# Moving a sample's and a recurrence's start to slots without weight splitting, transposing all first token pairs on TensorE, and starting the cache copies later

## The reference

```python
xn = _rmsnorm(x, g_pre)
u = xn @ w_in
gq, gk, gv, gg, glr, dq, dk, dv, dg, ga, gb = jnp.split(u, cuts, axis=-1)
# branch A: gated linear attention, in chunks of 64 tokens
b = jnp.cumsum(a_, axis=1)
q_in = q_ * jnp.exp(b)
att = jnp.where(causal, jnp.einsum('bihd,bjhd->bhij', q_in, k_ * jnp.exp(-b)), 0.0)
o = jnp.einsum('bhij,bjhe->bihe', att, v_) + jnp.einsum('bihd,bhde->bihe', q_in, s)
s = jnp.exp(b_end)[..., None] * s + jnp.einsum('bjhd,bjhe->bhde', k_end, v_)
# branch B: dilated windows; a sample reads its cache and the new rows
s = jnp.einsum('bthd,btkhd->bthk', q, kg) * (D ** -0.5)
o = jnp.einsum('bthk,btkhd->bthd', p / l, vg)
new_buf = jnp.stack([kk, vv], axis=2)[:, Lb + T - keep:]      # the caches moved on by 8 rows
# both
merged = jax.nn.sigmoid(ga) * y_a + jax.nn.sigmoid(gb) * y_b
h = x + _rmsnorm(merged @ w_out, g_post)
h = h + (pe @ w_ple_proj) * jax.nn.sigmoid(h @ w_ple_gate)
```

## Time and profile before

| | |
|---|---|
| median of 3 runs | 2871.57 us |
| the profiled execution | 2880.04 us, its span 2878.0 us |
| TensorE busy | 2671.1 us (93%) |
| VectorE, ScalarE, GpSimd busy | 1766.4 (61%), 1035.6 (36%), 432.4 us (15%) |
| DMA | 622.39 MB, mean 216 GB/s |

### The profile page before, as it was taken

The page is one execution under the profiler, slowest core; times in us unless marked ns, Lnnn a source line. Parts: engine busy times, 40 slices in busy tenths (PEclk is TensorE's granted clock), DMA queues, the critical chain, the costliest instruction groups (busy, mean ns, idle before and its releaser), DMA issues. The chain is left out here.

```text
span 2878.0 us, 54244 instructions
## 1 busy us (share of the span) xinstructions
PE 2671.1 (93%) x21916; PEld 2041.5 (71%) x21916; DVE 1766.4 (61%) x3181; ACT 1035.6 (36%) x1880; POOL 432.4 (15%) x649
## 2 busy tenths in 40 slices
PE   5786899899999989899999999999999999999998
PEld 4675787778887777778888888888887544444444
DVE  6475576666565665676667666766666455555552
ACT  4232244423222221222334444534423354444441
POOL 5131111121012212211112211011100000000000
PEclk8998999999999999999999999999999999999999
DMA  5798776698876779977756776455546976566652
GB/s 154 192 188 246 257 267 222 240 320 292 278 254 207 234 229 338 327 234 272 258 178 239 231 236 210 135 177 185 185 169 189 312 211 145 164 176 163 166 116 56
DMA packets 370059, 622.39 MB, mean 216 GB/s; under 512 B 199197, under 2 KB 204900, under 8 KB 365331
## 3 DMA queue, kind: packets, MB, share of 16 engines
q1 hardware_dynamic: 311554, 352.11, 39.8%
q0 software_dynamic: 44000, 233.26, 25.1%
q10 hardware_dynamic: 14256, 33.56, 3.2%
HBM read 429.15 MB, written 244.66 MB: 234 GB/s over the span
## 5 line engine op out<-in xcount | busy, mean ns | idle before, releaser
L853 PE MATMUL out<-w_hi,x_hi 128*128 128x256 f16 x3136 | 871.8, 278 | 67.6 <-DVE w_lo L709 23.9
L853 PE MATMUL out<-w_lo,x_hi 128*128 128x256 f16 x3136 | 871.5, 278 | 3.6 <-issue 3.6
L853 PE MATMUL out<-w_hi,x_lo 128*128 128x256 f16 x3136 | 871.0, 278 | 0.0
L775 DVE SCALAR_TENSOR_TENSOR stage<-out,stage 128x512 f32<-128x512 f32 (+1 forms) x567 | 378.8, 680 | 414.4 <-PE out L853 290.2
L853 PEld LDWEIGHTS out<-w_hi,x_hi 128*128 128x128 f16 x3136 | 313.0, 100 | 119.6 <-issue 28.7
L851 PE MATMUL out<-x_hi,w_hi 128*128 128x256 f16 x1344 | 372.7, 277 | 26.6 <-DVE w_lo L709 18.8
L851 PE MATMUL out<-x_hi,w_lo 128*128 128x256 f16 x1344 | 372.4, 277 | 0.0
L851 PE MATMUL out<-x_lo,w_hi 128*128 128x256 f16 x1344 | 372.0, 277 | 0.0
L705 ACT ACTIVATE w_hi<-raw 128x1024 f16<-128x1024 f32 x280 | 291.3, 1050 | 208.3 <-DVE raw L720 54.4
L709 DVE SCALAR_TENSOR_TENSOR w_lo<-raw,w_hi 128x1024 f16<-128x1024 f32 x280 | 346.0, 1240 | 9.5 <-ACT w_hi L705 9.4
L853 PEld LDWEIGHTS out<-w_lo,x_hi 128*128 128x128 f16 x3136 | 312.9, 100 | 46.3 <-issue 5.1
(11 more groups left out here) (354 smaller groups left out, 4267.3 us busy)
## 6 DMA issues: line engine op xcount, KB each, us to landing
raw<-in_w_in SPq DMA_DIRECT2D x80, 1024.0 KB, 8.1
out<-in_cache_kv_w POOLq DMA_DIRECT2D x64, 1020.0 KB, 9.4
U<-stage SPq DMA_DIRECT2D x224, 256.0 KB, 6.0
UT<-stage SPq DMA_DIRECT2D x96, 256.0 KB, 5.1
sw_vc<-in_cache_kv_w POOLq DMA_DIRECT2D x24, 1024.0 KB, 10.7
sw_kc<-in_cache_kv_w ACTq DMA_DIRECT2D x24, 1024.0 KB, 7.9
sw_rows<-U POOLq DMA_DIRECT2D x32, 512.0 KB, 7.0
out<-in_cache_kv_w POOLq DMA_DIRECT2D x16, 1008.0 KB, 8.1
```

The source lines that it names most:

```text
L775: return dve.scalar_tensor_tensor(out=out, in0=self.shaped(D, self.product(D, f, us), us), scalar=1.0 / W_SCALE, in1=other, op0=ALU.mult, ...
L853: return pe.matmul(out, x[:, 2 * d + u, f * HALF_K + k, :], w[:, k, :], start=start, stop=stop)
```

## The change

1. `BY_TENSOR` goes from 2 to 4: all four pairs of phase 0 are transposed by TensorE, 28 units of one form of one pair. A list, `BEFORE`, says ahead of which product each unit stands, and `kept_in` puts two units' `keep_hi` and `keep_lo` into each slot. DMA transposes remain for the sample tile and pairs 5 to 8, into a buffer of their own (`bounce`) in the place of a second set of rows. Squares and scaling of the first tiles move between the preludes and the first slots.
2. The forms are multiplied in the order P1, P2, P6, P7, P4, P5, P3 (before: P1, P6, P2, ...). The order in which weights are split stays P1, P2, P7, P6, P4, P5, P3.
3. GLA chunks of phase 0 start at slot 89 and on from there by a table (0, 7, 17, 24, ...), which is a tile's slot 4 or 11; those of phase 1 as before. The samples' recurrence goes from slot 163 to 166, the cutter of the later weights from 100 to 94.
4. The samples' attention starts at slot 258 and on from there by a table, each in a tile's slot 3.
5. The cache copies are issued with D 9 to 28 and 48 to 71 (88 pieces as before).

```diff
-P1, P6, P2, P7, P4, P5, P3 = range(FORMS)
+P1, P2, P6, P7, P4, P5, P3 = range(FORMS)
...
-GLA_SLOTS, GLA_PERIODS = (84, 625), (8, 7)
-GLA_SAMPLE_SLOT = 163
-SAMPLE_SLOT, SAMPLE_PERIOD = 264, 17
+GLA_SLOTS = (89, 625)
+GLA_STARTS = ((0, 7, 17, 24, 34, 41, 51, 58, 68), tuple(range(0, 57, 7)))
+GLA_SAMPLE_SLOT = 166
+SAMPLE_SLOT = 258
+SAMPLE_STARTS = (0, 17, 34, 51, 68, 85, 105, 125, 142)
...
-SHIFT_PAIRS = (range(3, 27), range(42, 62))
+SHIFT_PAIRS = (range(9, 29), range(48, 72))
-CUT_SLOT = 100
+CUT_SLOT = 94
...
-    BY_TENSOR = 2
+    BY_TENSOR = 4
...
-    LOAD_SLOTS = (7, 8, 13, 27)
+    LOAD_SLOTS = (9, 11, 15, 28)
+    BEFORE = [(5,), (6,), (7,), (8,), (9,), (10,), (11,), (12,), (13,), (14, 15), (16,), (17,), (18,), (19, 20), (21, 22), (23, 24), (25, 26), (27,), (), (), ()]
...
-        self.row = [[sb(f"row{s}{part}", [P, FORMS, BANK], F16) for part in "hl"] for s in range(2)]
-        self.bounce = [tile[:, :, :].rearrange("p f c -> p (f c)") for tile in self.row[1]]
+        self.row = [sb(f"row{part}", [P, FORMS, BANK], F16) for part in "hl"]
+        self.bounce = [sb(f"bounce{part}", [P, FORMS * BANK], F16)[:, :] for part in "hl"]
...
+    def pair_form(self, n):
+
+        return divmod(n, FORMS) if n < 2 * FORMS else (n % 2 + 2, n // 2 - FORMS)
...
+    def kept_in(self, slot):
+
+        return [self.pair_form(n) for n in range(FORMS, self.BY_TENSOR * FORMS) if (n - FORMS) // 2 == slot]
+
     def scalar(self, act, slot):
-        if 3 <= slot <= 6:
-            for f in (2 * (slot - 3), 2 * (slot - 3) + 1):
-                if f < FORMS:
-                    self.keep_hi(act, 1, f)
...
+        for k, f in self.kept_in(slot):
+            self.keep_hi(act, k, f)
...
-        for k, at in ((2, 4), (3, 7), (self.SAMPLE, 11)):
-            if slot == at:
-                self.turn_rows(sp, k)
+        if slot == 10:
+            self.turn_rows(sp, self.SAMPLE)
...
-        if pair < self.BY_TENSOR:
-            pe.wait_ge(self.lo_ready, pair * FORMS + f + 1)
-        elif f == P1:
-            self.wait_turned(pe, pair)
+        pe.wait_ge(self.lo_ready, self.unit(pair, f) + 1)
...
-                if D == 0:
-                    n = us[0] * FORMS + f + len(self.inputs.bank)
-                    if n < self.inputs.BY_TENSOR * FORMS:
-                        self.inputs.turn(pe, n // FORMS, n % FORMS)
+                if G == 0:
+                    for n in self.inputs.BEFORE[FORMS * (D + us[0]) + f + (FORMS if D else 0)]:
+                        self.inputs.turn(pe, n)
```

More of the change, by code:

```diff
@@ L357, in __init__ @@
         self.row_lo = one("row_lo")
-        self.row_turned = [one(f"row_turned{s}") for s in range(2)]
+        self.row_turned = one("row_turned")
         self.pairs_stored = one("pairs_stored")
@@ L539, in split_hi @@
             act.wait_ge(self.summed, self.sums_before(k + 1))
[L540 to L544, removed]
+        elif k > self.SAMPLE:
+            self.wait_turned(act, k - 1)
+        for dst, src in self.part_of(self.moves(k, self.row[0]), part):
             last = act.activation(dst, src, ACT.Copy)
@@ L548, in split_lo @@
     def split_lo(self, dve, k, part):
[L549 to L552, removed]
+        dve.wait_ge(self.row_hi, 2 * (k - self.SAMPLE) + part + 1)
+        his = [dst for dst, _ in self.part_of(self.moves(k, self.row[0]), part)]
+        for (dst, src), hi in zip(self.part_of(self.moves(k, self.row[1]), part), his):
             last = dve.tensor_tensor(dst, src, hi, ALU.subtract)
@@ L556, in turn_rows @@
     def turn_rows(self, sp, k):
[L557 to L560, removed]
+        sp.wait_ge(self.row_lo, 2 * (k - self.SAMPLE + 1))
+        rows, later = self.rows(self.tiles(k)[0]), k - self.SAMPLE - 1
         if later > 0:
@@ L602, in vector @@
     def vector(self, dve, slot):
[L603 to L610, removed]
+        if slot == 2:
             for i in self.tiles(3):
                 self.scale(dve, i)
-        if slot == 6:
+        for k, f in self.kept_in(slot):
+            self.keep_lo(dve, k, f)
+        if slot == 5:
             self.scale(dve, self.tiles(self.SAMPLE)[0])
-        for k, at in ((2, 2), (3, 5), (self.SAMPLE, 9)):
-            if slot in (at, at + 1):
-                self.split_lo(dve, k, slot - at)
+        if slot in (8, 9):
+            self.split_lo(dve, self.SAMPLE, slot - 8)
         for k in range(self.SAMPLE + 1, self.PREPS):
@@ L1147, in parts, with step @@
     def parts(self, r, phase):
-        p = GLA_PERIODS[phase]
-        def step(offset):
-            c, at = divmod(r - offset, p)
-            return phase * self.run + c if at == 0 and 0 <= c < self.run else None
+        starts = GLA_STARTS[phase]
+        begins, ends = starts[:-1], starts[1:]
+        def step(slots, slot):
+            return phase * self.run + slots.index(slot) if slot in slots else None
+        return step(begins, r), step(begins, r - 1), step(ends, r + 1), step(ends, r)
         return step(0), step(1), step(p - 1), step(p)
@@ L1206, in queue @@
     def queue(self, q, r, phase):
-        p, begin = GLA_PERIODS[phase], phase * self.run
+        begin, begins, ends = phase * self.run, GLA_STARTS[phase][:-1], GLA_STARTS[phase][1:]
         if r == -6:
@@ L1214, in queue @@
             self.load(q, begin)
-        c, at = divmod(r - 2 + p, p)
-        if at == 0 and 1 <= c < self.run:
-            self.load(q, begin + c)
-        c, at = divmod(r - p - 1, p)
-        if at == 0 and 0 <= c < self.run:
+        if r - 2 in begins[:-1]:
+            self.load(q, begin + begins.index(r - 2) + 1)
+        if r - 1 in ends:
+            c = ends.index(r - 1)
             c += begin
@@ L3132, in _ @@
                 inputs.keep_hi(act, 0, f)
-                if f in (P6, P7):
-                    for i in inputs.tiles(1 if f == P6 else 2):
+                if f in (P1, P6, P4):
+                    for i in inputs.tiles({P1: 1, P6: 2, P4: 3}[f]):
                         inputs.square(act, i)
@@ L3169, in _ @@
                 inputs.keep_lo(dve, 0, f)
-                if f == P2:
-                    for i in inputs.tiles(1):
+                if f in (P2, P4):
+                    for i in inputs.tiles({P2: 1, P4: 2}[f]):
                         inputs.scale(dve, i)
@@ L3204, in _ @@
             pe.wait_ge(inputs.identity_ready, 1)
-            for f in range(len(inputs.bank)):
-                inputs.turn(pe, 0, f)
+            for n in range(len(inputs.bank)):
+                inputs.turn(pe, n)
             for q in range(ALL_SLOTS):
```

67 lines of the change are left out of this document (31 added, 36 removed).

## The result

The changed kernel takes 2771.36 us, the median of 4 runs (2767.52 to 2778.78), against 2871.64 us before (4 runs): ratio 0.9653, 95% interval 0.9621 to 0.9685, or some 100 us. The forecast was 2745 us, its range 2700 to 2800.

A forecast was written before the change was run, and what follows sets the result against it. TensorE's idle time and lower clock in five stages bound it (span 2878.0 us, projection 2230). Terms −14 − 47 − 0 − 3 − 11 − 52 = −127 from 2880 give 2753, less 8.5: 2745 us, range 2700 to 2800.

The forecast's parts named there:

- signs of being wrong: `sw_sT` waits above 25 us, a 10 us wait in 110 to 338 us, or D 62 to 71 over 10 us longer.
- First tile: 0 to 110 us: 22.4 us of waits and slow clock gone, less 8.4 for 14 more TensorE units: −14 us.
- second rival: PE not at full speed in D1 (2770 us), and phase 1's transposes stalling by themselves (2767 us); chance 0.13.
- 110 to 338 us: Second stage: without cache copies, 57.9 us of idle and clock loss falls to 10.8: −47 us.
- an estimate of 2.5: Skill page's 350 to 400 GB/s applied to a 0.92 MB DMA transpose: about 2.5 us, against 4.14 measured alone.
- second half of the second rival: 110 to 338 us: phase 1's transposes stall by themselves, gaining −25 in place of −47: 2767 us.
- GLA and order of forms: Phase 0's GLA chunks at new starts, −3 us; P2 multiplied second in 570 to 864 us, −11 us.
- Samples: 864 to 1297 us: VectorE freed of splits and sums before the scores, query rows the new bound: −52 us.
- 13 of 64.8 us stay: Samples' stage: row fetches by GpSimd's queue still delay one or two samples, with small rests at others.
- Copies later: Cache copies at D 9 to 28 and 48 to 71 cost PE nothing: 0 us (ends −3, +10).
- third rival: D 62 to 71: copies share GpSimd's queue with phase 1's GLA chunk loads, 225 us lost: 2970 us; chance 0.03.

The follow-up runs named there:

- Both misses mended: Changed kernel with a sample's second step one slot earlier and the second group of cache copies at D 47 to 70: 2754.87 us, ratio 0.958.

## Why the prediction was right, and where it was off

The direction and the main causes were right, and the sum was off by 26 us. Two of the signs that it named did not show: PE still waits 4.2 us for a DMA transpose (the samples') in the first 100 us, and 18.7 us for `sw_sT` where 10 at most were expected. None of its signs of being wrong showed.

- **First tile: right** in size and, in the main, in mechanism (−14.2 for −14). The old inputs bring 10.8 us of it back and the old order of forms 3.0, which the prediction had not counted here. Transposes run at full clock among products, 0.60 us a unit; the second rival, built on their running slowly, falls. The page of the Trainium skill weighed there ("TensorE: Matmul & The Clock Gate", "Part 4: PE-mode transpose") is not borne out: in the kernel before the clock rose while PE had done transposes alone, and here units among products ran at full speed. (The transposes that open the changed kernel, with pauses between them, stayed at half, 0.42 us each.)
- **110 to 338 us: right in the main cause, too large in size.** The copies alone take 33 us from the old kernel where 47 were forecast. The table's −41.1 looks nearer because the first GLA chunk has left the stage; the prediction had not seen that this chunk's start, at slot 84, was among the stage's losses. The transposes don't stall by themselves (4.2 to 5.0 us), so the second half of the second rival falls too. The lone transpose's 4.14 us, which the prediction set against an estimate of 2.5, is the time for which the instruction held SyncE's queue; its data landed 6.4 us after its start. The sum does not use this number. The kernel's parts don't simply add here: undone in the new kernel, the copies cost 15 us in this stage, in D7 and not in D5, and by elimination that is due to the order of forms. That was not tried.
- **GLA and order of forms: too small in sum, and wrong in the split.** −3 and −11 were forecast; the stretch gave −13.1 with the first chunk moved into it, some −21 without. The order of forms is worth 32 us in the new kernel, not 11, for it also carries the tiles with GLA chunks, and the chunks' starts alone give nothing in splits. I had priced the order by the undisturbed tiles of one stage; there the price holds (D24 to D30, three tiles: 127.7 us before, 118.6 now).
- **Samples: the step that failed** is "13 of 64.8 us stay". VectorE's relief was counted rightly (the waits behind splits are gone, and undoing the slots costs 37.5 us). The fetch of rows was named as the new bound, but taken for one or two samples. VectorE waits for it in seven of eight: the fourth step's rows can only be fetched when the second step is done, and 7 us of landing don't fit into what is left. 18.7 us of waits stayed, where the mechanism was named but mis-sized; an earlier fetch took away 9.5 of them.
- **Copies later: "I take 0"** failed in one place. The copies' wait for products had kept GpSimd's queue from running ahead. Without it two loads met, for 6.6 us of idle time and a stretch at lower clock. I had looked for what the copies would meet at their new place, and not for what they had held back at the old one. The third rival (copies beside phase 1's GLA chunks) did not happen: D62 to D72 takes 280.6 us for 281.6.

Both misses mended, the kernel takes 2754.87 us, 10 us from the forecast. That closeness is partly luck, as two other terms were off in opposite directions (33 us for 47, and 21 for 14).

## What to carry to other kernels

An instruction that waits in an in-order queue also holds back what stands behind it: before moving it, ask what would then start earlier and what that would meet. When work is taken from an engine that others wait for, work out the next chain through every buffer of the ring (freed, fetched, landed, used) for each round, and not from one sample of it. Undo parts singly and look where the time comes back: the order of products, priced at 11 us in undisturbed tiles, was worth 32, as it also carries the tiles that other work had been moved into.

## What was unexpected in the hardware

A DMA transpose and plain copies that meet slow each other far more than their bytes would say. A transpose that holds the queue for 4.1 to 5.0 us and lands after 6.2 to 7.9 without copies beside it held it for 31.86 us and landed after 37.5 in the kernel before, and two copies of 1 MB issued 0.4 and 0.9 us behind it landed after 26 and 34 us (6 to 9 for the two just before it). DMA engines then showed a busy share of up to 1.14 at 145 GB/s, where another stretch with copies moved 319 GB/s at 0.90. In the changed kernel with the old copies one transpose held the queue for 13.89 us, and another for only 5.27 but landed after 22.6 us: the time on the queue does not tell how late the data are.
